# Two plain and 20 seven-product units per feed-forward stage in place of 4 and 18, with three sum buffers and new orders at the stage borders

## What is computed

```python
def swiglu(h, w1, w3, w2):
    return (jax.nn.silu(h @ w1) * (h @ w3)) @ w2      # h: 512 x 1024, w1, w3: 1024 x 2816, w2: 2816 x 1024
...
for layer in range(2):                                # first block
    ...                                               # attention and pooling, or a matrix LSTM
    x = x + g2 * swiglu(modulate(rms_norm(x), sh2, sc2), ffn_w1[layer], ffn_w3[layer], ffn_w2[layer])
...
x = x + 0.5 * swiglu_2(rmsnorm(x, ffn1_norm), ...)    # second block, once at its start
...
x = x + 0.5 * swiglu_2(rmsnorm(x, ffn2_norm), ...)    # and once at its end
```

## Time and profile before

| | |
|---|---|
| median of 3 runs | 2459.02 us (2455.99 to 2460.46) |
| the profiled execution | 2455.0 us, of which the span of the trace is 2453.2 us |
| PE busy | 2364.1 us, 96% of the span |
| PE weight loads busy | 2102.2 us |
| DVE busy | 1655.4 us, 67% |
| ACT busy | 1008.7 us, 41% |
| mean DMA rate | 132 GB/s |

### The profile page before, as it was taken

One profiled execution on the slowest core, in us unless ns is written; L12 is line 12 of the kernel. 1 busy time (PEld: TensorE's weight loads), 2 busy tenths in 40 slices (PEclk: granted clock), 3 DMA queues, 4 the chain that ended last, 5 costly groups with the idle time before them and its releaser, 6 DMA issues. The chain is left out here.

```text
span 2453.2 us, 35145 instructions
## 1 busy us (share of the span) xinstructions
PE 2364.1 (96%) x14848; PEld 2102.2 (86%) x14848; DVE 1655.4 (67%) x2005; ACT 1008.7 (41%) x1385; POOL 133.8 (5%) x153
## 2 busy tenths in 40 slices
PE   7989999999999999999999999999999999999998
PEld 6658899888799879998879998789989877899986
DVE  6687789667755667883368885446678544688844
ACT  3362444323344444442254442344556544444422
POOL 0210010000003000000000000000000000000000
PEclk9999999999999999999999999999999999999999
DMA  8215677564233136653236653222212222466521
GB/s 342 77 56 219 194 220 214 173 238 172 82 119 103 59 96 176 186 142 125 89 107 172 178 151 108 99 99 69 87 52 78 78 69 86 120 179 170 144 102 68
DMA packets 71726, 325.03 MB, mean 132 GB/s; under 512 B 7850, under 2 KB 9130, under 8 KB 49810
## 3 DMA queue, kind: packets, MB, share of 16 engines
q1 hardware_dynamic: 51984, 238.75, 28.0%
q0 software_dynamic: 16208, 78.13, 13.6%
q10 hardware_dynamic: 3378, 5.91, 0.9%
HBM read 320.52 MB, written 2.24 MB: 132 GB/s over the span
## 5 line engine op out<-in xcount | busy, mean ns | idle before, releaser
L240 PE MATMUL bank<-h_hi,w_hi 128*128 128x256 f32 (+1 forms) x1512 | 508.6, 336 | 21.0 <-DVE w_lo L917 10.7
L241 PE MATMUL bank<-h_lo,w_hi 128*128 128x256 f32 (+1 forms) x1512 | 499.6, 330 | 0.0
L242 PE MATMUL bank<-h_hi,w_lo 128*128 128x256 f32 (+1 forms) x1512 | 499.6, 330 | 0.0
L227 DVE TENSOR_TENSOR w_lo<-raw,w_hi 128x2048 fp32r<-128x2048 f32 x120 | 274.8, 2290 | 156.4 <-ACT w_hi L223 156.4
L240 PEld LDWEIGHTS bank<-h_hi,w_hi 128*128 128x128 f32 x1512 | 289.3, 191 | 55.5 <-issue 12.4
L240 PE MATMUL bank<-t_hi_tile,w_hi 128*128 128x256 f32 x1152 | 326.0, 283 | 0.0
L241 PE MATMUL bank<-t_lo_tile,w_hi 128*128 128x256 f32 x1152 | 326.0, 283 | 0.0
L242 PE MATMUL bank<-t_hi_tile,w_lo 128*128 128x256 f32 x1152 | 326.0, 283 | 0.0
L242 PEld LDWEIGHTS bank<-h_hi,w_lo 128*128 128x128 f32 x1512 | 289.4, 191 | 26.6
L241 PEld LDWEIGHTS bank<-h_lo,w_hi 128*128 128x128 f32 x1512 | 289.6, 192 | 25.6 <-issue 1.4
L240 PE MATMUL bank<-g_hi,w_hi 128*128 128x512 f32 x704 | 275.7, 392 | 8.3 <-DVE w_lo L227 6.3
(11 more groups left out here) (363 smaller groups left out, 4205.8 us busy)
## 6 DMA issues: line engine op xcount, KB each, us to landing
raw<-stream SPq DMA_DIRECT2D x120, 1024.0 KB, 4.9
raw<-stream SPq DMA_DIRECT2D x72, 512.0 KB, 5.5
work<-stream SPq DMA_DIRECT2D x72, 512.0 KB, 6.9
work<-stream POOLq DMA_DIRECT2D x72, 512.0 KB, 5.8
work<-stream POOLq DMA_DIRECT2D x19, 1024.0 KB, 7.9
raw<-stream SPq DMA_DIRECT2D x72, 256.0 KB, 6.4
h_plain<-stream POOLq DMA_DIRECT2D x16, 1024.0 KB, 5.8
work<-stream SPq DMA_DIRECT2D x13, 1024.0 KB, 12.3
```

Source lines behind the costliest of these rows:

```text
L227: nc.vector.tensor_tensor(w_lo[:, slot(m), :], raw[:, slot(m), :], w_hi[:, slot(m), :], ALU.subtract).then_inc(lo_split, 1)
L240: nc.tensor.matmul(out, stationary[0], moving[0], start=first, stop=False)
L241: nc.tensor.matmul(out, stationary[0], moving[1], start=False, stop=False)
L242: return nc.tensor.matmul(out, stationary[1], moving[0], start=False, stop=last)
```

## The change

`FFN_WHOLE` goes from 4 to 2, so a stage has 2 plain and 20 fast units. The steps that stood beside the plain units 0 to 3 move into the shadow of two. In ffn0 and ffn1 the sums of the activations and their split come first in DVE's and ACT's lists, ahead of the rescaling of plain unit 0; in ffn2 and ffn3 `hidden_scaled` comes first on ACT, and the sums stand between the two plain units. `whole_low(0)` now stands ahead of `make_further(0)`.

`mixes(r)` is a ring of three buffers in ffn1 to ffn3 (`depth`), two in ffn0. It has a semaphore of its own (`mixes_loaded`), SP issues it ahead of the unit's other parts, and POOL no longer waits for those. The last fast unit's further sums lie in the sum buffers and not in `raw`, and so the load of `md` waits for `further_low(FAST - 2)`. The loads of conditioning rows 24 to 31 move from POOL's queue to ACT's. Left out below are the definitions of semaphores, the list of which row waits on which, and three lines where `self.further` becomes `self.further(r)`.

```diff
@@ -40,7 +40,7 @@
 ADA_UNITS = 2 * 3 * KC
 ADA_ORDER = (0, 1, 2, 5, 3, 4)
 FFN_UNITS = FB + FB // 2
-FFN_WHOLE = 4
+FFN_WHOLE = 2
 
 
 PLAN = [("even_in", 5), ("even_out", 4), ("ffn0", FFN_UNITS), ("odd_in", 13), ("odd_out", 4),
...
@@ -212,7 +212,7 @@
             done = m // 2 + 1
             for name in ("ffn0", "ffn1", "ffn2", "ffn3"):
                 first = FIRST_UNIT[name] + FFN_WHOLE
-                done += 2 * sum(n % 2 == m % 2 for n in range(first, min(m + 1, first + FB - FFN_WHOLE)))
+                done += sum(n % 2 == m % 2 for n in range(first, min(m + 1, first + FB - FFN_WHOLE)))
             return 16 * done
 
         def split_hi(act, m, i=0):
...
@@ -371,6 +371,12 @@
                 self.norm.stay_busy(pe, 4, 2 * P)
                 self.sum_rows(pe, 0)
 
+
+        def load_ada(eng, n, held=None):
+            if held:
+                eng.wait_ge(ada_used, n + 1 - held)
+            eng.dma_start(conditioning.rows_of(n), stream[n:n + 1, :, :].rearrange("o p n -> p (o n)")).then_inc(
+                landing_of(n)[0], 16)
 
         class AdaBeside:
 
...
@@ -707,10 +714,10 @@
             CONV, HALF, QUARTER = FFN_WHOLE, S // 2, UNIT // 4
             silu = area(2048, 2, S)
             first, p1, u, z = area(2048, S), area(2560, HALF), area(3072, S), area(3584, S)
-            further = raw[:, :, 3 * (UNIT // 4):]
+            others = raw[:, :, 3 * (UNIT // 4):]
 
             def __init__(self, name, gate, norm, ada=False, shift_col=None):
-                self.ada, self.shift_col = ada, shift_col
+                self.ada, self.shift_col, self.depth = ada, shift_col, 2 if ada else 3
                 self.m0, self.gate, self.norm = FIRST_UNIT[name], gate, norm
                 self.md = self.m0 + FB
                 self.j0 = FB * ffns[0]
...
@@ -781,7 +788,18 @@
 
             def mixes(self, r):
 
-                return area((21504 if r < 2 else 4096) + UNIT // 2 * (r % 2), UNIT // 2)
+                n = UNIT // 2
+                return area(21504 + n * r if r < 2 else 4096 + n * ((r - 2) % self.depth), n)
+
+            def mixes_landed(self, r):
+
+                return 16 * (FAST // 2 * self.f + r // 2 + 1)
+
+            def further(self, r):
+
+                if r < FAST - 1:
+                    return self.others
+                return self.mixes(FAST - self.depth).rearrange("p (a n) -> p a n", a=2)
 
             def mixes_in(self, r):
 
...
@@ -804,36 +822,35 @@
             def load(self, sp, m):
 
                 q, r, s = self.QUARTER, m - self.fast(0), slot(m)
+                src = stream[place_of(m), :, :]
+                if r < 2:
+                    sp.wait_ge(h_ready, KC * self.norm.n + KC)
+                elif r < 2 + self.depth:
+                    sp.wait_ge(part_lo, self.hidden_lows(3))
+                else:
+                    sp.wait_ge(part_lo, self.part_low("mixes", r - self.depth))
+                if r >= 2:
+                    sp.wait_ge(mixes_loaded[s], self.mixes_landed(r - 2))
+                sp.dma_start(self.mixes(r), src[:, q:3 * q]).then_inc(mixes_loaded[s], 16)
                 sp.wait_ge(lo_split, m - 1)
-                src = stream[place_of(m), :, :]
+                if r == 2:
+                    sp.wait_ge(part_lo, self.part_low("s4", 0))
                 sp.dma_start(raw[:, s, 0:2 * q], src[:, 0:2 * q]).then_inc(landed[s], 16)
                 sp.dma_start(raw[:, s, 2 * q:3 * q], src[:, 3 * q:]).then_inc(landed[s], 16)
-                if r < 2:
-                    sp.wait_ge(h_ready, KC * self.norm.n + KC)
-                else:
-                    sp.wait_ge(part_lo, self.hidden_lows(3) if r < 4 else self.part_low("mixes", r - 2))
-                sp.dma_start(self.mixes(r), src[:, q:3 * q]).then_inc(landed[s], 16)
 
             def add_parts(self, pool, r):
 
                 q, s = self.QUARTER, slot(self.fast(r))
-                pool.wait_ge(landed[s], landings(self.fast(r)))
+                pool.wait_ge(mixes_loaded[s], self.mixes_landed(r))
+                if r >= 2:
+                    pool.wait_ge(mixed_in[s], self.mixes_in(r - 2))
                 pool.dma_start(self.mixes(r), stream[place_of(self.fast(r)), :, 2 * q:], accum_op=ALU.add).then_inc(
                     mixed_in[s], 16)
 
             def gpsimd(self, pool):
 
-                if self.ada:
-                    pool.wait_ge(ada_used, 24)
-                    pool.wait_ge(h_ready, KC * self.norm.n + KC)
-                    for n in range(24, 26):
-                        load_ada(pool, n)
                 for r in range(FAST):
                     self.add_parts(pool, r)
-                    if self.ada and r in (2, 4, 6, 8, 10, 14):
-                        n = 26 + (2, 4, 6, 8, 10, 14).index(r)
-                        pool.wait_ge(ada_used, n if n == 31 else n - 1)
-                        load_ada(pool, n)
 
             def hidden_scaled(self, act):
 
...
@@ -1029,6 +1046,8 @@
                 act.wait_ge(gated, self.j0 + 2 * d + 2)
                 if self.norm.deferred:
                     act.wait_ge(rows_scaled, self.pair_scaled(d))
+                if d == 0:
+                    act.wait_ge(part_lo, self.part_low("mixes", FAST - 1))
                 if d == 0 and self.ada:
                     act.wait_ge(conditioning.summed, 4)
                 if d:
...
@@ -1042,6 +1061,10 @@
 
 
             def scalar(self, act, st):
+                if self.norm.deferred:
+                    self.hidden_scaled(act)
+                else:
+                    self.hidden_high(act)
                 for j in range(self.CONV):
                     m, b = self.m0 + j, 2 * slot(self.m0 + j)
                     if self.norm.deferred:
...
@@ -1050,17 +1073,24 @@
                     else:
                         act.wait_ge(unit_used, m + 1)
                         nc.scalar.activation(self.silu[:, j % 2, :], bank[:, b, :], ACT.Silu).then_inc(silu_done, 1)
-                    if j < 2:
+                    if j < self.CONV - 2:
                         split_next_hi(act, m)
-                    if j == 0 and self.norm.deferred:
-                        self.hidden_scaled(act)
-                    if j == self.norm.deferred:
-                        self.hidden_high(act)
+                    if j == 0 and self.ada:
+                        act.wait_ge(ada_used, 24)
+                        act.wait_ge(h_ready, KC * self.norm.n + KC)
+                        for n in range(24, 26):
+                            load_ada(act, n)
                     if j == self.CONV - 2:
                         self.whole_high(act, 0)
+                        if self.norm.deferred:
+                            self.hidden_high(act)
                 self.mixes_high(act, 0)
                 for r in range(FAST):
                     self.further_high(act, r)
+                    if self.ada and r in (0, 2, 4, 6, 8, 12):
+                        n = 26 + (0, 2, 4, 6, 8, 12).index(r)
+                        act.wait_ge(ada_used, n if n == 31 else n - 1)
+                        load_ada(act, n)
                     if r:
                         self.apply(act, r - 1)
                     if r + 1 < FAST:
...
@@ -1098,17 +1128,20 @@
                                             ALU.mult).then_inc(gated, 1)
 
                 self.hidden_bias(dve)
+                if not self.norm.deferred:
+                    self.hidden_sums(dve, st)
+                    self.hidden_low(dve)
                 for j in range(self.CONV):
                     rescale(j)
-                    if j < 2:
+                    if j < self.CONV - 2:
                         split_next_lo(dve, self.m0 + j)
-                    if j == self.norm.deferred:
-                        self.hidden_sums(dve, st)
-                    if j == 1 + self.norm.deferred:
-                        self.hidden_low(dve)
                     if j == self.CONV - 2:
+                        if self.norm.deferred:
+                            self.hidden_sums(dve, st)
+                        self.whole_low(dve, 0)
+                        if self.norm.deferred:
+                            self.hidden_low(dve)
                         self.make_further(dve, 0)
-                        self.whole_low(dve, 0)
                         if self.ada:
                             conditioning.add_unit(dve, 3 * KC)
                 self.mixes_low(dve, 0)
...
@@ -3198,7 +3225,7 @@
                         ffn.load(sp, m)
                         return
                     if m == ffn.md or m == ffn.md + 1:
-                        sp.wait_ge(part_lo, ffn.part_low("further", FAST - 1))
+                        sp.wait_ge(part_lo, ffn.part_low("further", FAST - 2))
                 sp.wait_ge(lo_split, m - 1) if m >= 2 else None
                 sp.dma_start(raw[:, slot(m), :], stream[place_of(m):place_of(m) + 1, :, :].rearrange("o p n -> p (o n)")).then_inc(
                     landed[slot(m)], 16)
```

(9 more changed lines are left out.)

## The result

The changed kernel takes 2472.14 us (median of 5 runs, 2464.84 to 2475.28), the kernel before 2456.06 (5 runs, 2450.77 to 2460.46). The ratio is 1.0058, with a 95% interval of 1.0035 to 1.0082: slower, by some 0.6%. The forecast was 2468.5, in a range of 2457 to 2477. Its +9.6 us are a ratio of 1.0039, inside the interval, though near its lower end: the measured medians are 16.1 apart. The profiled execution took 2472.14, 17.1 more than that of before.

A forecast was written before the change was run, and what follows sets the result against it. TensorE, busy 96% of the span, was taken as the bound. 2455.0 - 6.4 + 28.4 + 6.4 - 5.9 - 4.0 - 1.6 - 7.3 = 2464.6; plus 4.0 from profiled run to median, said as 2468.5 us, range 2457 to 2477.

The forecast's parts named there:

- The entries: Start of each stage's fast units: TensorE idles 6.7, 6.2, 10.4 and 10.4 us, 28.4 us lost net of before.
- The clock there: Behind each entry's pause: one stretch of half clock, 1.6 us each, 6.4 us lost together.
- The bound of two stretches: Behind each entry's pause: upper bound of the clock term, two half-clock stretches where one was taken.
- Fast for plain: Units of all stages: eight plain units become fast, 10.88 to 10.08 us each, 6.4 us gained.
- Waits between fast units: Waits for mixed weights: end in ffn1 to ffn3 by a third buffer, 5.9 us gained; ffn0 gains 4.0 of 5.6.
- The rival in which ffn0's waits stay: ffn0's waits for mixed weights remain, since only the issuing queue changes: 5.6 us more, 2474; chance 0.08.
- Half clock in ffn0: Among ffn0's fast units: one stretch of half clock goes along with the waits for mixed weights, 1.6 us gained.
- Borders: Start of the down projection in ffn0 and ffn1: waits end, 2 x 2.05 us gained, plus 3.2 for half clock behind.

The follow-up runs named there:

- one_sum: The changed kernel with four of the five subtractions of each stage's activation sums left out, so output is wrong; 2443.22 us (one run).
- filled_entries: The changed kernel with useless matmuls on TensorE in the entry pauses, six in ffn0 and ffn1, eleven in ffn2 and ffn3; 2460.87 us (10 runs).
- two_buffers: The changed kernel with two sum buffers in all four stages; 2470.12 us (one run).
- mixed_part_last: four_plain with two sum buffers and the mixed part issued last of a unit's loads, as before the change; 2440.04 us (one run).
- late_first_down: The changed kernel with the down projection's first load held until the last fast unit's further split, as before; 2477.2 us (one run).
- four_plain: The changed kernel with four plain and 18 fast units again and the entry order of before; 2435.5 us (4 runs), ratio to before 0.9894.

## Why the prediction was right

**The entries, 28.4 us forecast.** Idle time 32.0, and 0.16 each from start to start, less 2 x 2.66 before: 27.3. ffn0 and ffn1 were worked out as 6.7 and 6.2, measured 6.02 + 0.16 each; ffn2 and ffn3 as 10.4, measured 10.0 + 0.16. In ffn0 the issues on ScalarE's queue cost nothing: they lie beside its copies, at 259.6. one_sum shows that the chain's length is the cause.

**The clock there, 6.4 forecast.** About 8 us measured, since the stretch behind the ten-microsecond pauses was 5.8 us of half clock and not 3.4. The bound of two stretches was nearer in ffn2 and ffn3 than the one that I took. That it is real cost, filled_entries shows. The rule of the Trainium skill that the prediction named ("TensorE: Matmul & The Clock Gate", section "Why this matters for your kernels") is borne out at all four entries by the 0.50 granted behind pauses of 6.0 and 10.0 us. The row that the prediction took it from was a weaker ground than it says: it stood behind a pause of 1.87 us, and the pauses of 2.50 us at the entries of ffn2 and ffn3 in the same trace had full clock behind them:

```profile
1283.70:1287.10 3.40, 3.40 (x29) 3.40 (x30) 2.44 (x4) 2.53 (x3) 0.00 (x0) 1.00 0.75 203
```

**Fast for plain, -6.4.** A fast unit still takes 10.08 us over all 20 in a row, and VectorE keeps up. This step stands.

**Waits between fast units, -9.9.** All of them went, 10.7 us of idle time and about 12 from start to start, those of ffn0 too (I took 4.0 of 5.6). The size was nearly right and the reason was wrong, so this term came out by luck: I gave ffn2 and ffn3 to the third buffer, and two_buffers has no such wait without it. Putting the mixed part first in the queue did some of it (mixed_part_last); what did the rest stays open. The rival in which ffn0's waits stay did not happen, though its mechanism, shared transfer engines, was not tested against another queue.

**Half clock in ffn0, -1.6.** Not gained. The stretch near 440 us is there in the changed kernel too, at 438, with no idle time before it but with the conditioning's sum, 32 matmuls of one column. In the kernel before that sum comes at 453.8, and full clock follows, so what brings the stretch stays open:

```profile
433.36 3.63 PE L343 MATMUL bank<-tab,work 128*128 128x1 f32 x32
...
438.10:441.40 3.30, 3.30 (x18) 3.30 (x17) 1.27 (x2) 0.01 (x1) 0.87 (x1) 0.50 0.79 205
```

**Borders, -4.1 and -3.2.** 4.1 went, as worked out, and late_first_down brings it back. The half clock behind the two of ffn0 and ffn1 went as well: their down projections last 119.87 us from first to last matmul, 121.5 and 121.6 before. But those of ffn2 and ffn3 got a stretch of their own, 121.6 for 120.0, behind the same wait of 2.2 us. The term of -3.2 came out at -0.2.

**The sum.** From the second plain unit's start to the down projection's, the four stages went from 227.7, 216.3, 222.9 and 222.2 us to 225.6, 220.3, 227.8 and 227.8: 12.4 more, where the forecast has 12.8 for the same stretch (9.6 without the -3.2 behind it). The difference to 17.1 lies outside: 4.7 more. None of it is in the down projections, which are 0.2 shorter together. 1.2 us are ahead of ffn0, where other runs of nearly the same program (two_buffers, filled_entries) don't have them, 1.3 between ffn0 and ffn1, 1.6 at the norm ahead of ffn2, where half clock lasts 6.8 us and not 3.4, and the rest behind that; the mean granted clock is 0.974 for 0.984 over the span.

The step that was mis-sized is thus the clock. The sum has 6.4 - 1.6 - 3.2 = 1.6 us for it. Measured are about 8 at the entries, nothing gained in ffn0, 0.2 gained at the borders, and by my estimate from the half-clock stretches some 3 more outside the stages: 9 too low. That the total was still near is in part luck, since the waits between fast units gave 2 us more than forecast and the entries' idle time 1.1 less; with the 1.2 us ahead of ffn0 that makes the step from 9.6 to 17.1, to half a microsecond. How much of the outside part belongs to the change stays open, since such stretches come and go between runs of kernels with the same waits.

## What to carry to other kernels

When work that is cheaper on the bound engine takes away the cover of a serial chain on other engines, price the chain against the cover first: here 1.6 us gained per stage (two units at 0.8) stood against 6 to 10 us of bare chain. The pauses of 6 and 10 us on TensorE cost 1.4 to 2.5 us more than their length, so add the half-clock stretch behind such a pause. The mends (load order, earlier release, order of two splits) were worth more than the change that came with them, and are best tried without it. When two edits aim at one wait, undo each alone before keeping the buffer.

## What the runs showed of the hardware

- The same wait of 2.22 us before the down projection is followed by half clock in some runs and not in others: 121.6 us for the 528 matmuls in the changed kernel and in four_plain, 120.0 in the kernel before and in filled_entries, and one of each in one_sum (ffn2 120.0, ffn3 121.4).
- A run of one-column matmuls with no idle time was followed by a stretch at a granted clock of 0.50 (at 438.1 us in the changed kernel). The same run was followed by full clock in the kernel before (at 457.5 us).
- Behind pauses filled with useless matmuls the granted clock was 1.00 and not 0.50, and with the real work starting no earlier the four fast stretches were 5.7 us shorter, the whole 11.3.
- The adding transfer's median from issue to landing was 8.3 us in the changed kernel and 5.8 with two buffers (two_buffers), each of 512 KB. With three buffers and four plain units (four_plain) it was 6.1; what makes the difference is not shown.
